# Side work ahead of the next weight split in every unrolled stage, and cross attention beside the units of its own projections, in a two-block kernel on one core

## The reference

```python
def memory_cross_attention(hn, mem_n, w_q, w_k, w_v, w_o):
    q = (hn @ w_q).reshape(b, s, XA_HEADS, XA_HEAD_DIM)
    k = (mem_n @ w_k).reshape(b, m, XA_HEADS, XA_HEAD_DIM)
    v = (mem_n @ w_v).reshape(b, m, XA_HEADS, XA_HEAD_DIM)
    logits = jnp.einsum("bshd,bmhd->bhsm", q, k).astype(jnp.float32) * (XA_HEAD_DIM ** -0.5)
    p = jax.nn.softmax(logits, axis=-1).astype(v.dtype)
    o = jnp.einsum("bhsm,bmhd->bshd", p, v).reshape(b, s, D_MODEL)
    return o @ w_o

h = h + memory_cross_attention(rmsnorm(h, norm_xa), rmsnorm(mem, norm_mem), xa_w_q, xa_w_k, xa_w_v, xa_w_o)
```

## Time and profile before

| what | value |
|---|---|
| time, median of 3 runs | 3383.43 us (3380.09 to 3383.83) |
| time of the profiled execution | 3385.29 us |
| span of the profiled execution | 3383.2 us |
| PE busy | 3199.5 us (95%) |
| DVE busy | 2073.8 us (61%) |
| ACT busy | 1568.0 us (46%) |
| granted TensorE clock, mean over the span | 0.974 |
| DMA | 662.63 MB, mean 196 GB/s |

### The profile page before, as it was taken

One profiled execution on the slowest core, in us unless ns is written; L12 is line 12 of the kernel. 1 busy time (PEld: TensorE's weight loads), 2 busy tenths in 40 slices (PEclk: granted clock), 3 DMA queues, 4 the chain that ended last, 5 costly groups with the idle time before them and its releaser, 6 DMA issues.

```text
span 3383.2 us, 58996 instructions
## 1 busy us (share of the span) xinstructions
PE 3199.5 (95%) x23728; PEld 3064.2 (91%) x23728; DVE 2073.8 (61%) x2461; ACT 1568.0 (46%) x1728; POOL 56.9 (2%) x52
## 2 busy tenths in 40 slices
PE   6999898999899996998999999998998999999997
PEld 5979787799779996988999989998988999999997
DVE  6567886667857766655654774456436665665444
ACT  5565443344443445443454754444434555554332
POOL 0000230000000000000000000000000000000000
PEclk8999998999999998999999999999999999999998
DMA  7887775478656863464566546665635556556653
GB/s 264 308 320 248 231 240 211 165 251 294 211 158 229 281 211 117 156 192 126 169 182 180 173 160 188 181 182 195 189 94 154 178 174 196 181 173 192 183 175 124
DMA packets 179549, 662.63 MB, mean 196 GB/s; under 512 B 20004, under 2 KB 20388, under 8 KB 178216
## 3 DMA queue, kind: packets, MB, share of 16 engines
q1 hardware_dynamic: 177704, 655.89, 60.2%
q10 hardware_dynamic: 1664, 4.19, 0.3%
HBM read 653.71 MB, written 6.29 MB: 195 GB/s over the span
## 4 chain that ended last, share of the span: by engine, by line
PE 85%; DVE 9%; ACT 2%; DVEq 1%; DMA 1%; issue 1%; ACTq 0%; SPq 0%
PE acc L669 23%; PE acc L673 23%; PE acc L671 23%; PE acc L680 4%; PE acc L682 4%; PE acc L681 4%; DVE w_lo L1675 3%; PE msc L630 1%; PE msc L628 1%; DVE mod_raw L1686 1%; DVE spare L2408 1%; PE msc L1052 0%; PE msc L779 0%; PE acc L831 0%; PE msc L810 0%
## 5 line engine op out<-in xcount | busy, mean ns | idle before, releaser
L1675 DVE TENSOR_TENSOR w_lo<-raw,w_hi 128x1024 fp32r<-128x1024 f32 x1020 | 1244.5, 1230 | 980.1 <-ACT w_hi L1126 973.4
L1126 ACT CAST w_hi<-raw 128x1024 fp32r<-128x1024 f32 x1020 | 1062.5, 1049 | 1278.8 <-PE acc L673 1012.8
L669 PE MATMUL acc<-a_hi,w_hi 128*128 128x256 f32 x4864 | 1389.2, 286 | 36.2 <-DVE w_lo L1675 13.0
L671 PE MATMUL acc<-a_lo,w_hi 128*128 128x256 f32 x4864 | 1381.8, 284 | 0.0
L673 PE MATMUL acc<-a_hi,w_lo 128*128 128x256 f32 x4864 | 1381.4, 284 | 0.0
L669 PEld LDWEIGHTS acc<-a_hi,w_hi 128*128 128x128 f32 x4864 | 939.3, 193 | 42.6 <-issue 32.1
L671 PEld LDWEIGHTS acc<-a_lo,w_hi 128*128 128x128 f32 x4864 | 939.5, 193 | 1.5
L673 PEld LDWEIGHTS acc<-a_hi,w_lo 128*128 128x128 f32 x4864 | 939.0, 193 | 0.0
L669 PE MATMUL acc<-b_hi,w_hi 128*128 128x256 f32 x1280 | 362.4, 283 | 0.0
L671 PE MATMUL acc<-b_lo,w_hi 128*128 128x256 f32 x1280 | 362.2, 283 | 0.0
L673 PE MATMUL acc<-b_hi,w_lo 128*128 128x256 f32 x1280 | 362.2, 283 | 0.0
(11 more groups left out here) (317 smaller groups left out, 2537.3 us busy)
## 6 DMA issues: line engine op xcount, KB each, us to landing
raw<-in_w_ffn_up SPq DMA_DIRECT2D x176, 512.0 KB, 4.4
mod_raw<-in_w_mod SPq DMA_DIRECT2D x128, 512.0 KB, 4.8
raw<-in_w_ffn_down SPq DMA_DIRECT2D x88, 512.0 KB, 3.7
ada_raw<-in_w_ada SPq DMA_DIRECT2D x64, 512.0 KB, 5.9
raw<-in_w_xa_k SPq DMA_DIRECT2D x32, 512.0 KB, 4.9
raw<-in_w_xa_v SPq DMA_DIRECT2D x32, 512.0 KB, 5.1
raw<-in_w_k SPq DMA_DIRECT2D x32, 512.0 KB, 4.6
raw<-in_w_v SPq DMA_DIRECT2D x32, 512.0 KB, 4.9
```

The lines of the kernel that those rows point to most:

```text
L669: pe.matmul(out, wh, hi[:, kc, :], start=(begin and m % 2 == 0), stop=False, skip_group_check=True)
L671: pe.matmul(out, wh, lo[:, kc, :], start=False, stop=False, skip_group_check=True)
L1126: nc.scalar.copy(w_hi[:, slot], source).then_inc(hi_done, 1)
L1675: vec.tensor_tensor(w_lo[:, slot], source, w_hi[:, slot].bitcast(F32), ALU.subtract).then_inc(lo_done, 1)
```

## The change

It has two parts. In every unrolled stage, `side(j)` on ACT and on DVE now stands ahead of the split of unit j + 4 (behind the epilogue's first half; its second half comes after the split, as before). And xa_q and xa_o are unrolled stages of four groups; the four heads' attention is their side work. `head_at(j)` counts the units of both stages together: head h has its logits and softmax at unit 8h + 9, its transposes at 8h + 10, and its product with the values at 8h + 11. So heads 0 to 2 stand in xa_q, and head 3 at units 1 to 3 of xa_o, whose first three groups of b chunks are ready before.

```diff
@@ the table of stages @@
-    Stage("xa_q", "w_xa_q", "F", 2, act=1),
-    Stage("xa_o", "w_xa_o", "F", 2, act=2, dve=2),
+    Stage("xa_q", "w_xa_q", "F", 1, groups=4, act=1),
+    Stage("xa_o", "w_xa_o", "F", 1, groups=4, act=2, dve=2),
...
+def head_at(j):
+
+    h, step = divmod(j - (DC // KU + 1), DC // KU)
+    return (h, step) if 0 <= h < XA_H and step < 3 else (None, None)
@@ PE @@
-            run("xa_q", a_hi, a_lo, PAIR["mix_out"], batch=2)
-
-            pe.wait_ge(act_done, ACT_DONE["xa_q"])
-            pe.wait_ge(xa_in, 32)
...
-            logits(0)
-            for h in range(XA_H):
-                if h + 1 < XA_H:
-
-                    steps.wait(act=XaStep.exponentials(h))
-                    logits(h + 1)
...
+            def attention(first):
+
+                def side(j):
+                    h, step = head_at(first + j)
+                    if step == 0:
+                        if h == 0:
+                            pe.wait_ge(xa_in, 32)
+
+                        pe.wait_ge(act_done, ACT_DONE["xa_q"] - (XA_H - 1 - h))
+                        if h:
+
+                            steps.wait(act=3 * h - 2)
+                        for tt in range(2):
+                            for kc in range(4):
+                                mm = pe.matmul(msc[:, 0, tt * T:(tt + 1) * T], xa_qf[:, 4 * h + kc, tt * P:(tt + 1) * P],
+                                               xa_kf[:, 4 * h + kc, :], start=(tt == 0 and kc == 0), stop=(kc == 3),
+                                               skip_group_check=True)
+                        steps.done(mm)
+                    if step == 1:
+
+                        steps.wait(dve=2 * h + 2)
...
+                    if step == 2:
+
+                        steps.wait(act=3 * h + 2)
...
+            run("xa_q", a_hi, a_lo, PAIR["mix_out"], batch=2, side=attention(0))
+            run("xa_o", b_hi, b_lo, PAIR["xa"], batch=4, side=attention(STAGE["xa_q"].n))
@@ ACT and DVE: walk @@
-        def walk(stage, i, split, epilogues, last=False, side=None, window=None):
+        def walk(stage, i, split, epilogues, last=False, side=None, window=None, early=False):
...
                 rest = epilogues[kind](i, g, i * stage.n + (stage.u0 + j + 1 + RING)) if ends else None
+                if early:
+                    side(j)
                 if not (last and j + RING >= stage.n):
                     split(stage, i, j + RING)
                 for r in rests:
                     r()
                 rests = [rest] if rest else []
-                if side:
+                if side and not early:
                     side(j)
...
-                    walk(stage, i, split, epilogues, side=side)
+                    walk(stage, i, split, epilogues, side=side, early=bool(side))
@@ DVE @@
+            def attention(first):
+
+                def side(j):
+                    h, step = head_at(first + j)
+                    if step == 0:
+
+                        steps.wait(pe=3 * h + 1)
+                        vec.tensor_reduce(soft[:, 0:2], msc[:, 0, :].rearrange("p (a b) -> p a b", a=2), AX, ALU.max)
+                        dve.drain()
+                        steps.done(vec.tensor_scalar(soft[:, 2:4], soft[:, 0:2], -(XA_D ** -0.5), None, ALU.mult))
+
+                        steps.wait(act=3 * h + 1)
+                        vec.reciprocal(soft[:, 6:8], soft[:, 4:6])
...
+            run("xa_q", none(), side=attention(0))
+            run("xa_o", residual(1.0), side=attention(STAGE["xa_q"].n))
```

More of the change, by code:

```diff
@@ L1016, in _ @@
             steps.end("xa_pair")
-            run("xa_q", a_hi, a_lo, PAIR["mix_out"], batch=2)
-            pe.wait_ge(act_done, ACT_DONE["xa_q"])
-            pe.wait_ge(xa_in, 32)
-            def logits(h):
-                for tt in range(2):
-                    for kc in range(4):
-                        mm = pe.matmul(msc[:, 0, tt * T:(tt + 1) * T], xa_qf[:, 4 * h + kc, tt * P:(tt + 1) * P],
-                                       xa_kf[:, 4 * h + kc, :], start=(tt == 0 and kc == 0), stop=(kc == 3),
-                                       skip_group_check=True)
-                steps.done(mm)
@@ L1575, in _ @@
             pair(a_hi, "xa_pair")
-            run("xa_q", to_slab(xa_qf))
-            def exponentials(h):
-                steps.wait(dve=2 * h + 1)
-                for tt in range(2):
-                    mm = nc.scalar.activation(prob[:, tt, :], msc[:, 0, tt * T:(tt + 1) * T], ACT.Exp,
-                                              bias=soft[:, 2 + tt:3 + tt], scale=XA_D ** -0.5,
-                                              accum_out=soft[:, 4 + tt:5 + tt])
-                steps.done(mm)
@@ L1589, in _ @@
-            exponentials(0)
-            for h in range(XA_H):
-                steps.wait(pe=XaStep.turned(h))
-                steps.done(nc.scalar.copy(flat(prob_t), msc[:, 1, :]))
-                if h + 1 < XA_H:
-                    exponentials(h + 1)
-                steps.wait(pe=XaStep.result(h))
-                steps.done(nc.scalar.copy(b_hi[:, 4 * h:4 * h + 4, :].rearrange("p a b -> p (a b)"),
-                                          msc[:, 2:4, :].rearrange("p a b -> p (a b)")))
@@ L1600, in _ @@
-            steps.end("attention")
-            run("xa_o", with_squares(to_buffer(ACT.Copy)))
+            def attention(first):
+                def side(j):
+                    h, step = head_at(first + j)
+                    if step == 0:
+                        steps.wait(dve=2 * h + 1)
+                        for tt in range(2):
+                            mm = nc.scalar.activation(prob[:, tt, :], msc[:, 0, tt * T:(tt + 1) * T], ACT.Exp,
+                                                      bias=soft[:, 2 + tt:3 + tt], scale=XA_D ** -0.5,
+                                                      accum_out=soft[:, 4 + tt:5 + tt])
+                        steps.done(mm)
+                    if step == 1:
+                        steps.wait(pe=3 * h + 2)
+                        steps.done(nc.scalar.copy(flat(prob_t), msc[:, 1, :]))
+                    if step == 2:
+                        steps.wait(pe=3 * h + 3)
+                        steps.done(nc.scalar.copy(b_hi[:, 4 * h:4 * h + 4, :].rearrange("p a b -> p (a b)"),
+                                                  msc[:, 2:4, :].rearrange("p a b -> p (a b)")))
+                        if h == XA_H - 1:
+                            steps.end("attention")
+                return side
@@ L1602, in _ @@
+            run("xa_q", to_slab(xa_qf), side=attention(0))
+            run("xa_o", with_squares(to_buffer(ACT.Copy)), side=attention(STAGE["xa_q"].n))
             rms("ffn_norm")
@@ L2488, in _, with attention, side @@
-            steps.end("attention")
-            run("xa_o", residual(1.0))
+            def attention(first):
+                def side(j):
+                    h, step = head_at(first + j)
+                    if step == 0:
+                        steps.wait(pe=3 * h + 1)
[4 more added lines that the diff above has]
+                        vec.reciprocal(soft[:, 6:8], soft[:, 4:6])
+                        dve.drain()
+                        for tt in range(2):
+                            mm = vec.tensor_scalar(prob[:, tt, :], prob[:, tt, :], soft[:, 6 + tt:7 + tt], None, ALU.mult)
+                        steps.done(mm)
+                    if step == 2:
+                        steps.wait(act=3 * h + 3)
+                        vec.tensor_tensor(b_lo[:, 4 * h:4 * h + 4, :].rearrange("p a b -> p (a b)"),
+                                          msc[:, 2:4, :].rearrange("p a b -> p (a b)"),
+                                          b_hi[:, 4 * h:4 * h + 4, :].bitcast(F32).rearrange("p a b -> p (a b)"),
+                                          ALU.subtract).then_inc(pair_ready, 1)
+                        if h == XA_H - 1:
+                            steps.end("attention")
+                return side
```

60 lines of the change are left out of this document (16 added, 44 removed).

## The result

The changed kernel takes 3362.4 us (median of 4 runs, 3361.0 to 3365.5), the kernel before 3383.6 us beside it: a ratio of 0.9941, with a 95% interval of 0.9924 to 0.9958. The ratio is that of the means and gives 20 us; the medians are 21.2 us apart. The forecast was 3361.0.

What follows compares the result with a forecast made beforehand. PE bounds the kernel, with a matmul under way for 95% of the span, so only its waits and half-clock stretches pay. The terms sum to -22.4 us, from the median 3383.4 to 3361.0; range 3354 to 3371.

Steps and rivals of the forecast that it cites:

- Attention, -10.1: Between xa_q and xa_o: 10.85 us of waits and slow clock go, 0.3 more is covered, softmax waits cost 1.0.
- ends of matmuls that nothing covers now: In the attention's four heads: matmul ends that a weight unit will cover, estimated at 0.3 us in all.
- The start, -7.3: Kernel start, mem_k: squares ahead of the fifth ada unit's split bring PE's first weight unit from 43.5 to 36.2 us.
- sgu_u, -4.7: Before the SGU's mixing: most of PE's 3.14 us wait goes (-2.9), and the 16 matmuls run at full clock (-1.7).
- rnn_x, -1.2: PE's 6.90 us wait for the retention's third normalised chunk has one split fewer ahead of it, 1.23 us.
- merge_a, -1: DVE bounds this stretch and keeps its work, only the order changes: -1 us, between -3 and +2.
- mem_v, +1.0: A split now behind the lambda terms makes PE wait 3.5 us, an old 1.8 us wait goes; +1.0 taken.
- the rings behind are fuller by then: In mem_v: the reason given for taking +1.0 us where the waits alone left +1.7.
- Group ends, +0.9: Group ends with a mod_sum now ahead of a split: lat_k +1.2, a give-back behind ctx_k's end -0.5, ctx_k's first +0.2.
- Unrolling, 0: In xa_q and xa_o: PE is busy through every loop turn, so removing the two loops gains nothing.
- rival 2: Unrolled xa_q and xa_o each meet one instruction fetch stall, +4.6 us together, giving 3365.6; 12%.
- Rival 4: Slower: side work ahead of a split drains the ring at 20 group ends, +30 us, giving 3391; 3%.

Runs made afterwards that it cites:

- e7: The changed kernel with each head's transposes and product with the values one unit later; 3355.8 us, ratio 0.9925 to the kernel before.
- e3: The kernel before with side work ahead of the split in mem_k alone; 3378.0 us, ratio 0.9981.
- e8: The changed kernel with the four small constants issued behind the memory's first quarter instead of its fourth; 3359.9 us, ratio 0.9928 to the kernel before.
- e4: The kernel before with side work ahead of the split in sgu_u alone; 3378.9 us, ratio 0.9987.
- e1: The changed kernel with side work ahead of the split in xa_q and xa_o only; 3371.7 us, ratio 0.9968 to the kernel before.
- e6: The changed kernel with each mod_sum again behind the split of its step; 3357.7 us, ratio 0.9921 to the kernel before.

## Why the prediction was right, point by point

**Attention, -10.1: right in kind, 2.2 us too small.** The wait for the probabilities was given as 0.2 to 0.25 us a head, and is 0.33; that two units in place of one remove it (e7) shows its cause. What was mis-sized first is the "ends of matmuls that nothing covers now", estimated at 0.3 us in all. From unit to unit, a head adds 3.27 us with its logits, 0.86 with its transposes and the wait, 3.35 with its product, and 0.18 to the unit behind that, 7.65 in all and 30.6 for four, where the prediction has 31.0 - 0.3 + 1.0 = 31.7. The block's rows count each matmul group to its modelled end: a group of 16 shows 3.62 and adds 3.27. Before, the block cost 41.85 us and the same 0.18 behind it, so the attention itself gave 11.4. The other 0.9 of the stages' 12.3 is not the attention's. Some 0.4 is the end of xa_o, where PE waits 4.12 us for the next norm's sums in all nine kernels with xa_o unrolled and 4.51 in all five with the loop; the rest stands at the start of xa_q, whose first two units take 8.0 us in mean with the loops and 7.5 unrolled, either with a scatter of 0.7 or more, and just behind xa_o, by the clock after the wait.

**The start, -7.3: -5.3.** The step that failed is the end of the sums, put at 27.2, and a preloaded table: they end near 28.8 (1.6 us), and the table's load comes behind them (0.4 us more), so that the reciprocal is done at 30.69 + 1.75 = 32.4 and not at 30.45. From there PE's first unit comes 6.1 us later, as before, not 5.75. "What is gained at its head stays at its end" held (e3). The constants' landing (15.7 against 16.28) was right, and, as e8 shows, beside the point.

**sgu_u, -4.7: -4.6, partly by luck.** The wait held: it is gone (e4), and 3.1 us with it. Its size was read a little high, since PE is still busy for 0.28 of the 3.14 us of that window, and waits 2.87. The clock held only in part: that PE without a wait mixes at full clock came true in all, but the half clock that it was to save, 1.7 us, is not there in every execution of the order as before (1.00 in e1), and the mean of -4.6 hangs on which three profiles were taken.

**rnn_x, -1.2: -1.2,** as worked out: PE's wait is 1.13 us shorter. **merge_a, -1: -1.5,** as merge_a 3.7 longer and rnn_y 5.4 shorter: the order moved work over the stage's end. Why its order pays wasn't tested.

**mem_v, +1.0: +1.4.** The wait of 3.5 us came as worked out (3.40), and the old one of 1.8 us went. That "the rings behind are fuller by then" was the weak step. What the sum left out is the clock, on both sides: the slow units behind the old wait went (some 1.7 us), and slow ones came behind the new wait (0.2 to 2.6 us).

**Group ends, +0.9: about +0.4,** inside the scatter of these stages, so not shown; by PE's waits alone it is -0.6 (e6's table). The give-back at the wait behind ctx_k's end was too small in the prediction: +1.1 there and -2.0 in lat_k, for -0.5. At lat_k's end PE's wait grew by 0.36 us and not by 1.2. One reason is that DVE is done with the convolution earlier against PE: 0.57 us ahead of the end of PE's last matmul in the changed kernel, 0.52 behind it in before. The other is that the mod_sum took 1.21 us and not 1.75, though GpSimd was at work. The timelines of DVE and of GpSimd in the changed kernel:

```profile
465.42 1.21 DVE L1691 SCALAR_TENSOR_TENSOR mod_raw<-mod_raw,cond_wide 128x1024 f32<-128x1024 f32 x1
...
469.56 1.75 DVE L1691 SCALAR_TENSOR_TENSOR mod_raw<-mod_raw,cond_wide 128x1024 f32<-128x1024 f32 x1
```

```profile
463.43 0.83 POOL L1651 TENSOR_TENSOR gate_tmp<-gate_tmp 64x256 f32<-64x256 f32 x1
...
465.42 1.80 POOL L1651 TENSOR_TENSOR gate_tmp<-gate_tmp 64x256 f32<-64x256 f32 x1
...
469.15 1.08 POOL L1651 TENSOR_TENSOR gate_tmp<-gate_tmp 64x256 f32<-64x256 f32 x1
```

Both start at 465.42, and there it is GpSimd's instruction that takes 1.80 us (0.83 for the same operation at 463.43) and the mod_sum has its usual length (mean 1.245). Four us later GpSimd's starts first, at 469.15, and takes 1.08, and the mod_sum, from 469.56, takes 1.75. So the price of a meeting doesn't always fall on DVE. It fits the Trainium skill ("SBUF — State Buffer", section "SBUF: two separate sides"), by which the one that starts first holds the shared pair of ports for its whole instruction.

**Unrolling, 0: some -0.4,** the shorter wait at xa_o's end told above, which stands in each of the nine unrolled kernels; no run unrolls these stages and does nothing else, so the cause is open. No new wait of PE's sequencer appeared within xa_q or xa_o, so rival 2 is out; ffn_down has its one as before (2.29 us at 3211.44). Rival 4, the drained ring, is real in small: in mem_v, where two ada units come to each weight unit and DVE has little time to spare, and with 1.1 and 0.4 us at the ends of ctx_k and lat_k.

The errors cancel: 2.2 at xa_q and xa_o and some 1 at the small places on one side, the start's 2.0 and mem_v's 0.4 on the other. The total is nearer than its terms deserve, and that is luck.

## What to carry to other kernels

Where an engine's queue mixes work for later (a split four units ahead) with work that someone waits for now, put the second first; what it costs showed here where the engine had little time to spare (mem_v, the ends of ctx_k and lat_k), so look at the places where its share is near full before moving a long step there. A releaser that the profile names is not yet the bound: ask what ends next if it comes earlier, as for the constants and the second square. And a serial chain of short steps on several engines is best laid between units of a long product, with as many units between two steps as the chain needs. Where a gain counts on the clock, as at the mixing, one profile of before isn't enough: read the same place in several.

## What was not expected of the hardware

Kernels whose PE code in a stage is the same differ there by up to 6 us, much of it by how soon the clock comes back. In lat_q and the mLSTM behind it (111.2 to 117.4 us over all kernels, none of which changes a PE instruction there) PE waits some 9 us and then runs small matmuls. In the changed kernel's profile the granted clock is 0.50 and 0.58 in the next 10 us, and the stage takes 115.3 us; in e7's it is 0.69 and 1.00, and the stage takes 111.4. Windows of the one, then of the other:

```profile
552.30:562.10 9.80, 0.22 (x4) 0.13 (x3) 9.60 (x20) 5.35 (x5) 0.00 (x0) 0.59 0.74 254
562.10:567.00 4.90, 4.89 (x11) 3.06 (x11) 0.00 (x0) 0.00 (x0) 0.00 (x0) 0.50 0.58 215
567.00:572.00 5.00, 5.00 (x13) 3.41 (x13) 1.02 (x2) 0.91 (x2) 0.00 (x0) 0.58 0.00 0
```

```profile
551.00:559.70 8.70, 0.19 (x4) 0.10 (x2) 8.54 (x18) 4.82 (x5) 0.00 (x0) 0.59 0.73 275
559.70:564.70 5.00, 4.94 (x14) 3.66 (x15) 0.69 (x2) 0.03 (x2) 0.00 (x0) 0.69 0.61 210
564.70:569.70 5.00, 5.00 (x23) 3.85 (x23) 1.29 (x2) 1.79 (x4) 0.00 (x0) 1.00 0.00 0
```

The instructions ahead of both are the same, the first windows are 9.8 and 8.7 us long and nearly all idle, and the length of the wait alone doesn't decide it: e4, after 9.75 us without a matmul, has 0.72 and 1.00 in the next 10 us, and before, after 9.79, has 0.50 and 0.58. What decides when the clock rises these runs don't show. The same holds for the three smaller places above: the mixing in sgu_u, the unit behind the wait of 3.40 us in mem_v, and the unit behind the 4x4 transposes. It is why a profile's span alone tells no effect under 5 us here, while PE's waits at a place, or the length of a stage that doesn't scatter by itself, do.
